# Linear attention on one core: chunk outputs as tokens by values, the norm by token, the gate beside its own head's chain; RWKV heads alternating, transposes 128x128

## The reference, cut to what matters

```python
def step(S, inp):                      # RWKV, per token and head; S is value x key
    sa = jnp.einsum('bhvk,bhk->bhv', S, -kk_t)
    S = S * w_t + sa[..., None] * (kk_t * a_t) + v_t[..., None] * k_t
    return S, jnp.einsum('bhvk,bhk->bhv', S, r_t)

def step(S, inp):                      # GLA, per chunk of 64 tokens
    A = jnp.einsum('bhtd,bhsd,bhtsd->bhts', qc, kc, decay)
    o = jnp.einsum('bhts,bhsv->bhtv', A, vc) + jnp.einsum('bhtk,bhkv->bhtv', qc * jnp.exp(b), S)
    S = jnp.exp(b_last) * S + jnp.einsum('bhsk,bhsv->bhkv', kc * jnp.exp(b_last - b), vc)
    return S, o
out = rmsnorm(out, gn).reshape(B, T, GLA_VW) * jax.nn.silu(r)
```

## Time and profile before

| | us |
|---|---|
| median of 3 runs | 4171.99 (4170.81 to 4173.69) |
| the profiled execution | 4163.56 |
| its span, first to last instruction | 4161.9 |
| RWKV's heads, 168 to 891 us | 723 |
| GLA's phases -1, 0, 1, 2, 3 with 4 | 117, 146.4, 147.1, 147.1, 96.5 |

### The profile page before, as it was taken

The page is one execution under the profiler, slowest core; times in us unless marked ns, Lnnn a source line. Parts: engine busy times, 40 slices in busy tenths (PEclk is TensorE's granted clock), DMA queues, the critical chain, the costliest instruction groups (busy, mean ns, idle before and its releaser), DMA issues. The chain is left out here.

```text
span 4161.9 us, 62269 instructions
## 1 busy us (share of the span) xinstructions
PE 3737.7 (90%) x26087; PEld 3159.1 (76%) x26087; DVE 1467.3 (35%) x2652; ACT 795.6 (19%) x1415; POOL 533.4 (13%) x356
## 2 busy tenths in 40 slices
PE   6698988889787865999999998999995999999996
PEld 4466676765445644999999995677674999999996
DVE  2334535333246654332223233113313332322322
ACT  1121111101035632311111112212210321111110
POOL 0000000000400001422212220000000422222221
PEclk9799998889879987999999999999995999999998
DMA  2000000010420012111111102001102111111102
GB/s 92 13 12 12 12 18 11 7 75 23 110 70 1 1 69 88 48 53 33 54 36 45 41 30 102 30 33 36 60 25 116 59 47 46 52 33 46 51 30 98
DMA packets 76592, 189.20 MB, mean 45 GB/s; under 512 B 30932, under 2 KB 45204, under 8 KB 73380
## 3 DMA queue, kind: packets, MB, share of 16 engines
q1 hardware_dynamic: 63588, 157.97, 11.3%
q0 software_dynamic: 8448, 27.27, 2.1%
q10 hardware_dynamic: 4352, 1.05, 0.2%
HBM read 161.34 MB, written 29.04 MB: 46 GB/s over the span
## 5 line engine op out<-in xcount | busy, mean ns | idle before, releaser
L224 PE MATMUL ps<-ff_x,ff_wh 128*128 128x384 f32 (+1 forms) x3960 | 774.9, 328 | 0.0
L224 PEld LDWEIGHTS ps<-ff_x,ff_wh 128*128 128x128 f32 x3960 | 668.8, 188 | 0.8
L224 PE MATMUL ps<-ff_x,ff_wl 128*128 128x384 f32 (+1 forms) x2112 | 465.5, 328 | 0.0
L224 PEld LDWEIGHTS ps<-ff_x,ff_wl 128*128 128x128 f32 x2112 | 360.8, 188 | 0.0
L519 DVE TENSOR_TENSOR resid<-resid,ps 128x384 f32 (+1 forms) x240 | 113.2, 527 | 383.8 <-PE ps L224 383.8
L2343 PE MATMUL ps<-act,gl_w 128*128 128x384 f32 (+1 forms) x768 | 245.6, 481 | 0.0
L224 PE MATMUL ps<-ff_hh,ff_dh 128*128 128x384 f32 (+1 forms) x1056 | 233.1, 328 | 4.6 <-DVE ff_hl L511 4.6
L224 PE MATMUL ps<-ff_hh,ff_dl 128*128 128x384 f32 (+1 forms) x1056 | 232.7, 328 | 0.0
L224 PE MATMUL ps<-ff_hl,ff_dh 128*128 128x384 f32 (+1 forms) x1056 | 232.7, 328 | 0.0
L2343 PEld LDWEIGHTS ps<-act,gl_w 128*128 128x128 f32 x768 | 148.5, 195 | 91.1 <-issue 9.5
L1657 PE MATMUL ps<-rw_up,rw_low 64*64 64x128 f32 (+1 forms) x1632 | 147.5, 271 | 46.3 <-DVE rw_tri L2029 31.3
(11 more groups left out here) (549 smaller groups left out, 6143.1 us busy)
## 6 DMA issues: line engine op xcount, KB each, us to landing
ff_w<-in_wg SPq DMA_DIRECT2D x44, 512.0 KB, 3.5
ff_w<-in_wu SPq DMA_DIRECT2D x44, 512.0 KB, 3.5
ff_wd<-in_wd POOLq DMA_DIRECT2D x48, 256.0 KB, 3.0
ff_wd<-in_wd POOLq DMA_DIRECT2D x32, 320.0 KB, 3.3
ns_past<-in_cache_slc SPq DMA_DIRECT2D x64, 128.0 KB, 2.1
rw_w<-in_w_rwkv SPq DMA_DIRECT2D x14, 512.0 KB, 3.5
np_w<-in_w_nsa SPq DMA_DIRECT2D x8, 652.0 KB, 7.9
resid<-in_x SPq DMA_DIRECT2D x1, 4352.0 KB
```

The source lines that it names most:

```text
L224: mm = pe.matmul(g.ps[:, bank + c, 0:n], w[:, k, :], x[:, o:o + n], start=(first and i == 0), stop=(last and i == 2))
```

## The change

RWKV: the matmuls of the two heads of a pair stand alternately; the four 64x64 transposes per chunk and head become transposes of 128 partitions by up to 128 columns, five per two chunks, and ScalarE copies each block to its place. GLA: the stationary operand of `products_out` is now the chunk's own matrix and the decayed query, the moving one the values and the state, so that an output tile holds 128 tokens by 256 values; for the sample tokens the queries are masked by GpSimd (`qe8`). ScalarE takes squares and sums by token as it copies; VectorE scales by token; PE transposes the scaled tile (N0 to N4), and VectorE multiplies gain and gate as it takes the result from PSUM. R of head h moves from phase h-1 to phase h; F steps stand between the R steps.

```diff
                     t = slice(64 * (c0 + c), 64 * (c0 + c) + 64)
+                    art = ar[:, c0 + c, :, :].rearrange("p a t -> p (a t)")
+                    for x, left in enumerate((bt, kt)):
+                        for h in halves:
+                            o = 256 * (c % 2) + P * x
+                            pe.matmul(g.ps[h, c // 2, o:o + P], left[h, t], art[h, :], start=True, stop=True)
                     for h in halves:
-                        at, art = ar[h, c0 + c, 0, :], ar[h, c0 + c, :, :].rearrange("p a t -> p (a t)")
-                        tri = g.ps[h, c // 2, 256 * (c % 2):256 * (c % 2) + 256]
-                        pe.matmul(tri[:, 0:P], bt[h, t], art, start=True, stop=True)
-                        pe.matmul(tri[:, P:2 * P], kt[h, t], art, start=True, stop=True)
-                        pe.matmul(g.ps[h, 6, 64 * c:64 * c + 64], at, bt[h, t], start=True, stop=True)
-                        for x, src in enumerate((at, bt[h, t], kt[h, t], v[h, t])):
-                            o = 256 * (c % 2) + 64 * x
-                            mm = pe.matmul(g.ps[h, 3 + 2 * (c // 2), o:o + 64], src, g.id2[h, :], start=True, stop=True)
+                        pe.matmul(g.ps[h, 6, 64 * c:64 * c + 64], art[h, 0:64], bt[h, t], start=True, stop=True)
+                for q in reversed(range(0, n, 2)):
+                    m = min(2, n - q)
+                    t = slice(64 * (c0 + q), 64 * (c0 + q + m))
+                    if m == 2:
+                        both = ar[:, c0 + q:c0 + q + 2, :, :].rearrange("p c a t -> p (c a t)")[:, 64:192]
+                        pe.transpose(g.ps[:, 3 + q, 0:P], both, g.ident)
+                    pe.transpose(g.ps[0:64, 3 + q, 0:P], ar[:, c0 + q, 0, :], g.ident)
+                    for x, src in enumerate((bt, kt, v)):
+                        mm = pe.transpose(g.ps[0:64 * m, 3 + q, P * x + P:P * x + 2 * P], src[:, t], g.ident)
                 s.scored.mark(mm)
...
-                if level == 0:
+                if level == 6 or (level == 0 and n > 2):
                     s.tokens.next(pe)
...
-                for h in halves:
-                    if i == 4:
-                        for q in range(NB):
-                            ps = g.ps[h, BANK[0], 64 * q:64 * q + 64]
-                            pe.matmul(ps, b.m8[h, 2, q, :], b.u[h, :], start=True, stop=False)
-                            pe.matmul(ps, b.m8[h, 1, q, :], tok[h, c, 3, :], start=False, stop=False)
-                            mm = pe.matmul(ps, g.id2[h, :], b.st8[h, q, :], start=False, stop=True)
-                    else:
-                        ps = g.ps[h, 7, 64:P]
-                        pe.matmul(ps, tok[h, c, 1, :], b.u[h, :], start=True, stop=False)
-                        mm = pe.matmul(ps, tok[h, c, 2, :], tok[h, c, 3, :], start=False, stop=True)
+                if i == 4:
+                    for q in range(NB):
+                        ps = g.ps[:, BANK[0], 64 * q:64 * q + 64]
+                        for h in halves:
+                            pe.matmul(ps[h, :], b.m8[h, 2, q, :], b.u[h, :], start=True, stop=False)
+                        for h in halves:
+                            pe.matmul(ps[h, :], b.m8[h, 1, q, :], tok[h, c, 3, :], start=False, stop=False)
+                        for h in halves:
+                            mm = pe.matmul(ps[h, :], g.id2[h, :], b.st8[h, q, :], start=False, stop=True)
...
+                    for h in halves:
+                        mm = pe.matmul(ps[h, :], tok[h, c, 2, :], tok[h, c, 3, :], start=False, stop=True)
                 s.s_ready.mark(mm)
...
+                    pe.matmul(py[h, :], b.u[h, :], tri[h, c, 1, :], start=True, stop=False)
+                for h in halves:
+                    pe.matmul(py[h, :], tok[h, c, 3, :], tri[h, c, 3, :], start=False, stop=False)
+                if i == 4:
+                    for q in range(NB):
+                        for h in halves:
+                            mm = pe.matmul(py[h, :], b.st8[h, q, :], b.m8[h, 1, q, :], start=False, stop=(q == NB - 1))
+                else:
+                    for h in halves:
+                        mm = pe.matmul(py[h, :], b.st[j % 2][h, :], b.ar[j % 2][h, c0 + c, 1, :], start=False, stop=True)
...
+                for q in reversed(range(0, n, 2)):
+                    turned = g.ps[:, 3 + q, :].rearrange("p (x h t) -> p h x t", x=4, h=2)
+                    for p in range(min(2, n - q)):
+                        for h in range(2):
+                            a = act.activation(b.tok[ring(j, i)][halves[h], q + p, :, :], turned[halves[p], h, :, :], ACT.Copy)
+                    s.tokens.mark(a)
...
-    tail = ["V8", "R0", "S9", "R1", "R2", "R3", "R4", "R5"] + [f"F{t}" for t in range(9)]
-    project = ("L0 L1 L2 S1 K0 K1 S2 K2 Q0 S3 Q1 Q2 S4 V0 V1 S5 V2 V3 S6 V4 V5 S7 V6 V7 S8").split() + tail
+    soft, shifted, exped, keys, rooted, scaled = signal.soft, signal.shifted, signal.exped, signal.keys, signal.rooted, signal.scaled
+    outer, o_ready, o_out, state, kt8_ready, qe8_ready = signal.outer, signal.o_ready, signal.o_out, signal.state, signal.kt8_ready, signal.qe8_ready
+    first = "G0 G1 G2 L0 L1 L2 K0 K1 K2 Q0 Q1 Q2 V0 V1 V2 V3 V4 V5 V6 V7 V8 F0 F1 F2 F3 F4 F5 F6 F7 F8"
+    middle = ("S0 L0 L1 L2 S1 K0 K1 N0 N1 S2 K2 N2 N3 N4 Q0 S3 Q1 Q2 S4 V0 V1 S5 V2 V3 S6 V4 V5 S7 V6 V7 S8 V8 R0 S9 "
+              "R1 F0 F1 R2 F2 F3 R3 F4 F5 R4 F6 F7 F8 R5")
+    fourth = "S0 N0 N1 N2 S1 N3 N4 R0 S2 R1 S3 R2 S4 R3 S5 R4 S6 S7 R5 S8 S9"
+    last = "N0 N1 N2 N3 N4"
 
     def sequence(h):
-        chain, new, done = 0 <= h < 4, h + 1 < 4, 0 <= h - 1 < 4
-        names_ = ["S0"] + (["N0", "N1", "N2"] if done else []) + (["G0", "G1", "G2"] if h == -1 else []) + project
-        return [x for x in names_ if (chain if x[0] == "S" else new if x[0] not in "N" else True)]
+        listed = (first if h < 0 else middle if h < 3 else fourth if h == 3 else last).split()
+        return [x for x in listed if h >= 1 or x[0] != "N"]
...
+    by_vector = lambda x: x[0] in "LFN"
...
-                    sp.dma_start(b.w[0][:, :, :], d.w_gla_r[2 * n]).then_inc(here[0], 16)
+                    sp.dma_start(b.w[0][:, :, :], d.w_gla_qk[5] if h < 0 else d.w_gla_r[2 * h]).then_inc(here[0], 16)
...
-                        sp.dma_start(d.gla_out[:, 2 * q + x, :], b.o[q % 2][:, x, :]).then_inc(o_stored, 16)
+                    consumed(sp, h, "N4")
+                    sp.dma_start(d.gla_out[:, 2 * q:2 * q + 2, :], b.o[:, :, :]).then_inc(o_stored, 16)
                 if q == 2:
-                    sp.wait_ge(o_stored, 96)
...
                     full(sp, h, "Q2")
-                    sp.dma_start(b.w[1][:, :, :], d.w_gla_r[2 * n + 1]).then_inc(here[1], 16)
...
+                if 0 <= h < 3:
                     full(sp, h, "R2")
-                    sp.dma_start(b.w[0][:, :, :], d.w_gla_qk[4 + n + 1]).then_inc(here[0], 16)
...
             for h in range(4):
+                pool.wait_ge(keys.sem, h + 1)
+                if h:
+                    pool.wait_ge(o_ready.sem, 9 * h)
+                qe8_ready.mark(pool.tensor_tensor(b.qe8[:, :, :], b.qe[h % 2][:, NP:TOK].unsqueeze(1).to_broadcast([P, NB, NS]), g.bcol, ALU.mult))
...
+                out = g.ps[:, 2 + (9 * h + t) % 2, 0:256]
+                if 9 * h + t >= 2:
                     o_out.next(pe)
                 if t < 8:
-                    for c in range(2):
-                        hr = slice(64 * c, 64 * c + 64)
-                        for x in range(2):
-                            p = g.ps[:, 2 + c, 64 * x:64 * x + 64]
-                            pe.matmul(p, v[hr, t, P * x:P * x + P], at[hr, t, :], start=True, stop=False)
-                            mm = pe.matmul(p, b.st[:, (2 * t + c + h) % 4, P * x:P * x + P], qe[:, t * P + 64 * c:t * P + 64 * c + 64], start=False, stop=True)
+                    two = [slice(64 * c, 64 * c + 64) for c in range(2)]
+                    for hr in two:
+                        pe.matmul(out[hr, :], at[hr, t, :], v[hr, t, :], start=True, stop=False)
+                    for c, hr in enumerate(two):
+                        mm = pe.matmul(out[hr, :], qe[:, t * P + 64 * c:t * P + 64 * c + 64], b.st[:, (2 * t + c + h) % 4, :], start=False, stop=True)
                 else:
+                    pe.matmul(out[0:NS, :], at[0:NS, 8, :], v[0:NS, 8, :], start=True, stop=False)
                     pe.wait_ge(st_here, 16 * (h + 1))
-                    for x in range(2):
-                        p = g.ps[:, 2, P * x:P * x + 64]
-                        pe.matmul(p, v[0:NS, 8, P * x:P * x + P], at[0:NS, 8, :], start=True, stop=False)
-                        for r in range(NB):
-                            mm = pe.matmul(p[:, 8 * r:8 * r + 8], b.st8[:, r, P * x:P * x + P], qe[:, NP + 8 * r:NP + 8 * r + 8],
-                                           start=False, stop=(r == NB - 1))
+                    qe8_ready.next(pe)
+                    for r in range(NB):
```

(81 more changed lines are left out.)

80 lines of the change are left out of this document (27 added, 53 removed).

## The result

The changed kernel takes **3938.78 us** (median of 4, 3937.91 to 3943.38) against 4172.84 for the kernel before: a ratio of 0.944 [0.9424, 0.9457]. The forecast was 3988, the range 3935 to 4045: right in sign and inside the range, but the gain was 49 us larger than forecast. The profiled execution took 3937.91 us, its span is 3936.2.

A forecast was written before the change was run, and what follows sets the result against it. PE, 90% busy, was taken as the only engine near full. Gains of 75.5 us in RWKV and 108 in GLA, off the profiled 4163.6 and with 8.4 added back, gave 3988 us; range 3935 to 4045.

The forecast's parts named there:

- Scores: RWKV scores: a group falls from 6.73 to 4.27 us, 2.46 less; 44.5 us over all groups.
- 6 of them: RWKV scores: six changes between 64-row and 128-row tiles a group, about 0.16 us each, 0.96 in all.
- ScalarE's copies: RWKV scores: two copies of 1.09 us become eight of perhaps 0.3, 0.2 us longer in sum, costed at nothing.
- Sample group: RWKV sample group: alternating heads halve 10 us of matmuls per pair to 5; 28 us gained over four pairs.
- Rival 3: RWKV and GLA: the clock rises as overlapped halves fill starved arrays; 35 us more gain, 3953 us; chance 0.12.
- Rival 2: RWKV: half the gain doesn't arrive because VectorE could come last; 38 us lost, 4026 us; chance 0.14.
- Rival 4: RWKV and GLA: the granted clock falls as PE gets idler; at 0.72 the whole takes 4253 us; chance 0.03.
- Rival 1: RWKV and GLA: array halves don't run beside each other in the new places; 97 us lost, 4085 us; chance 0.03.
- Phases 0 to 2: GLA phases 0 to 2: S tiles 31.7, S8 7, dense matmuls behind it 13.5, N 3.4; 55.6 us gained.
- the three stretches behind S8: GLA: dense matmuls at half clock, 13.7 us in each of three phases, finish in about 9; 13.5 us gained.
- R's move: GLA: R's 29.2 us leave phase -1; phases 3 and 4, where PE idles, still fall from 96.5 to 71.7, gaining 24.5.
- Rival 5: GLA phase 3: R's steps don't cover the chain; up to 25 us return, 4013 us; within the forecast's chance of 0.68.

The follow-up runs named there:

- the faster versions: Changed kernel with R0 ahead of N0 and R5 ahead of S7: 3927.34 us; then also the last head's scaling ahead of S9's add: 3929.66 us.
- GLA's narrow products: Changed kernel with each product of a GLA output tile in four pieces of 64 columns, for t below 8: 3974.67 us (0.9539).

## Why the prediction was right, and where it was short

**Scores: a term sized too small.** 44.5 us were forecast, and the 20 groups went from 129.4 to 61.6 us, 67.8 less. The 14 groups at full clock gave 3.50 each where 2.46 were forecast, 14.6 of the 23.3 us that were missing. The largest part is the step "6 of them" for the changes of shape: the code has 2 a group, all matmuls first and then all transposes, and four changes fewer at 0.147 us are 0.6 (the price, 0.16, was right). A further 0.2 is that the old group, taken as 8 x 0.84 = 6.73, measured 6.90 between its first and last start alone; the last 0.2 or so is not assigned. The two groups at the lower clock gave 15.6 where 9.8 were forecast, since the changed ones stood there only in part, and the four small groups 3.2 where 0.3 were. That all of it reaches the end was right.

**ScalarE's copies were misread, without harm.** The 1.09 us of the earlier trace rows are the time of both old copies together, not of each, and the eight new ones take 3.12: 2.0 us longer, not 0.2. No wait of PE for them stands among the stage's waits after the change, so that costing them at nothing was right.

**Sample group: right.** 28 forecast; `through`, `update` and y of the four pairs went from 53.5 to 22.1 us, 31.4 less, and undoing the alternation cost 28.5.

**The rest of RWKV**, about 16 us, against 3 for y. It goes with 95 us less at the lower clock, of which 49 lie in the two terms above; the other 46 would give at most 23. Rival 3, the clock rises, was given 0.12 and came true beside the forecast, not in its place: its 35 us and the forecast's terms should have been added up.

**Rival 2, VectorE binds, fell**: its idle time before the masks shrank by 66.2 us over all groups (142.8 to 76.6), nearly PE's whole saving of 67.8, and was not used up. **Rival 4, the clock falls, fell**: it rose in both stages.

**Rival 1 fell**: in the scores the first matmuls of both heads start 6 ns apart (484.941 and 484.947 us), though they stand on different rows of the array and write into one PSUM bank, on different partitions. The two chunks of a GLA tile (L2376) also stand on different rows and write into one bank: the pair takes 0.58 us, change of shape included, where one after the other its four passes alone would take 0.86 (an estimate from the dense passes of the earlier trace rows). That is against the sentence of the Trainium skill (TensorEngine Tiling (Array Packing), Gotcha 1: PSUM Pressure) that different row tiles can't access the same bank at the same time. The measurement decides; both cases have the outputs on different partitions.

**Phases 0 to 2**: 71.3 us less (440.7 to 369.4, from first outer product to first outer product), 55.6 forecast. S tile 1.80 (1.92 forecast), S8 4.17 (4.2): right. The clock was the mis-sized term: only the three stretches behind S8 were counted, 13.5, while 68.3 us at the lower clock became 6.8. PE is busy in nearly all of that, so it costs half its length: 34.1 and 3.4, a gain of 30.7 from the clock. The other 40.6 us are shorter work, for which 42.1 were forecast.

**R's move: a right sum from a wrong reason.** Phase -1 lost 29.3 us (29.2 forecast), phases 3 and 4 20.8 (24.5). But the prediction said that R fills PE's idle time there. It adds 27.0 to a chain that without it takes 52.1, so of its 29.2 us only some 2 are covered. The sum came out because it counted R's 29.2 in full beside the rest of the chain. Rival 5 had this part right, that R covers hardly anything, but no time came back with it. What made room were the shorter products, the small reciprocals and the clock, which came without the move too. Of the 47.8 us between the old last phases (99.9) and those without R, about 23 are the clock: PE had matmuls in flight for 57.0 us at the lower level in the one and 10.9 in the other, and half of the difference is 23. How the rest divides was not tried. Up to the next stage's first load the last phases took 79.1 us, where 71.7 + 3.4 were forecast; 3.3 us of wait for the first scaled tile and 2.75 for the last are where the faster versions found their time. Two small slips in the prediction's sums change nothing: 96.5 less 71.7 is 24.8, not 24.5, and its slow bounds add up to 4041, not 4038.

**What stays open** is why the clock rose, and that is much of the gain. Time with matmuls in flight at the lower clock fell from 131.0 to 49.2 us in RWKV and from 129.6 to 22.6 in GLA. If each such microsecond counts half, that is 41 of RWKV's 115 us and 54 of GLA's 121, at most, since PE does not set the pace everywhere. PE's idle time does not explain it. In the first 79.4 us of phase 3 the old kernel had matmuls in flight for 64.1, and stood at the lower clock for 69.9. Without R, the new products left PE idle for 19 of 51.6 us, at a granted clock of 0.85. A slower clock makes matmuls last longer, but with the busy time at the lower clock counted half the old kernel is still the busier one, 70% against 59%. Changes of shape alone did not do it in GLA. A kernel with only the old 8-column sample products was not tried, nor one with the old tile orientation alone.

## What to carry to other kernels

Count how many passes in a row go to the same part of the array. In these kernels PE overlapped neighbours by itself where that was six (3.67 us against 3.40), and hardly where it was 48 (5.41 against 2.80): there, alternate by hand. Gather matmuls of one tile shape: here two changes a group in place of eight saved 0.88 us. Before a step is moved to fill a gap, ask what the gap is once the other edits are in. A term that depends on the clock belongs in the sum, with its bounds, rather than in a rival.

## What the runs showed of the hardware that was not expected

- The next head's matmuls start while the last three passes of the head before are still to come, ahead of their place in the program (in the scores and in `through`; 3.67 us against 3.40 for a group).
- A change between 64-row and 128-row tiles costs 0.147 us in RWKV's scores and 0.14 in GLA's narrow products.
- Matmuls on different rows of the array write into one PSUM bank, on different partitions, 6 ns apart and without a loss of pace.
- The same code of one stage took 738 to 749 us, and RWKV 607.6, 612.5 and 614.4, with 55, 70 and 68 us at the lower clock. A single profile can't carry a difference under 10 us between kernels in such a stage. A stage that the clock leaves alone can: GLA's phase 1 took 122.8 us in all nine kernels that have the changed GLA code as it stands up to there.
